# RWKV head products as pairs of 64x64 matmuls on quarters of the array, and both layers written out

## The reference

```python
def step(state, inp):
    r_t, w_t, k_t, v_t, a_t, b_t = inp
    sa = jnp.einsum('bhvk,bhk->bhv', state, a_t)
    state = state * w_t[:, :, None, :] + sa[..., None] * b_t[:, :, None, :] \
            + v_t[..., None] * k_t[:, :, None, :]
    return state, jnp.einsum('bhvk,bhk->bhv', state, r_t)
_, y = lax.scan(step, state0, xs)
```

## Time and profile before

| | us |
|---|---|
| runs: median (lowest to highest of 3) | 1418.83 (1415.55 to 1419.67) |
| profiled execution: span, first to last instruction | 1412.0 |
| PE busy / PEld busy | 1340.1 (95%) / 1273.3 (90%) |
| DVE busy / ACT busy | 885.5 (63%) / 604.4 (43%) |
| mean granted TensorE clock | 0.961 |

### The profile page before, as it was taken

One profiled execution on the slowest core, in us unless ns is written; L12 is line 12 of the kernel. 1 busy time (PEld: TensorE's weight loads), 2 busy tenths in 40 slices (PEclk: granted clock), 3 DMA queues, 4 the chain that ended last, 5 costly groups with the idle time before them and its releaser, 6 DMA issues.

```text
span 1412.0 us, 28243 instructions
## 1 busy us (share of the span) xinstructions
PE 1340.1 (95%) x10414; PEld 1273.3 (90%) x10434; DVE 885.5 (63%) x1518; ACT 604.4 (43%) x904; POOL 47.7 (3%) x31
## 2 busy tenths in 40 slices
PE   7999999979989989999979999999799999999998
PEld 6999998958978879999979999998589788999998
DVE  4666666686653665666656666666866537566665
ACT  3444445545432234444444444455554323344442
POOL 3000000021000000000000000000210000000000
PEclk8999999989999979999989999999899899799999
DMA  5656665510010226665535666655100103366653
GB/s 156 179 179 183 187 184 135 161 57 1 1 45 1 66 86 180 184 185 179 165 109 176 181 185 182 189 130 141 45 2 1 45 1 105 90 182 186 182 179 118
DMA packets 243396, 174.59 MB, mean 124 GB/s; under 512 B 10274, under 2 KB 228540, under 8 KB 243324
## 3 DMA queue, kind: packets, MB, share of 16 engines
q1 hardware_dynamic: 243324, 173.64, 41.6%
HBM read 172.57 MB, written 1.05 MB: 123 GB/s over the span
## 4 chain that ended last, share of the span: by engine, by line
PE 80%; DVE 10%; issue 5%; ACT 2%; DMA 1%; SPq 0%; DVEq 0%; ACTq 0%
PE bank L1294 20%; PE bank L1295 19%; PE bank L1296 19%; PE bank L1565 3%; PE bank L1546 2%; DVE wlo L753 2%; PE bank L1557 2%; PE bank L1311 1%; PE bank L1336 1%; PE bank L1521 1%; PE bank L1301 1%; ACT whi L542 1%; DVE xlo L783 1%; PE bank L1625 1%; DVE root L769 1%
## 5 line engine op out<-in xcount | busy, mean ns | idle before, releaser
L753 DVE TENSOR_TENSOR wlo<-raw,whi 128x1024 fp32r<-128x1024 f32 x324 | 394.7, 1221 | 270.7 <-ACT whi L542 269.4
L1294 PE MATMUL bank<-xhi,whi 128*128 128x256 f32 x1840 | 535.0, 291 | 18.5 <-DVE xlo L783 14.7
L1295 PE MATMUL bank<-xlo,whi 128*128 128x256 f32 x1840 | 527.8, 287 | 0.0
L1296 PE MATMUL bank<-xhi,wlo 128*128 128x256 f32 x1840 | 527.7, 287 | 0.0
L542 ACT ACTIVATE whi<-raw 128x1024 fp32r<-128x1024 f32 x324 | 338.3, 1049 | 299.9 <-PE bank L1296 266.4
L1294 PEld LDWEIGHTS bank<-xhi,whi 128*128 128x128 f32 x1840 | 360.8, 196 | 25.8 <-DVE xlo L783 17.7
L1295 PEld LDWEIGHTS bank<-xlo,whi 128*128 128x128 f32 x1840 | 361.1, 196 | 0.1
L1296 PEld LDWEIGHTS bank<-xhi,wlo 128*128 128x128 f32 x1840 | 360.6, 196 | 0.0
L1294 PE MATMUL bank<-hhi,whi 128*128 128x256 f32 x704 | 202.8, 288 | 0.1
L1295 PE MATMUL bank<-hlo,whi 128*128 128x256 f32 x704 | 201.9, 287 | 0.0
L1296 PE MATMUL bank<-hhi,wlo 128*128 128x256 f32 x704 | 201.7, 287 | 0.0
(11 more groups left out here) (229 smaller groups left out, 1375.1 us busy)
## 6 DMA issues: line engine op xcount, KB each, us to landing
raw<-in_ffn_w_gate_dram SPq DMA_DIRECT2D x88, 512.0 KB, 3.9
raw<-in_ffn_w_up_dram SPq DMA_DIRECT2D x88, 512.0 KB, 3.9
raw<-in_ffn_w_down_dram SPq DMA_DIRECT2D x88, 512.0 KB, 3.3
raw<-in_w_in_dram SPq DMA_DIRECT2D x34, 512.0 KB, 4.0
raw<-in_w_out_dram SPq DMA_DIRECT2D x16, 512.0 KB, 3.4
raw<-in_w_in_dram SPq DMA_DIRECT2D x8, 256.0 KB, 3.2
raw<-in_w_q_up_dram SPq DMA_DIRECT2D x4, 384.0 KB, 3.6
work<-in_x_dram SPq DMA_DIRECT2D x1, 1024.0 KB, 6.6
```

The lines of the kernel that those rows point to most:

```text
L753: V_.tensor_tensor(wlo[:, b.slot, 0:width], raw[:, b.slot, 0:width], whi[:, b.slot, 0:width].bitcast(F32), ALU.subtract).then_inc(lo_ready, 1)
L1294: mm(out, hi, mhi, start=start, stop=False, **kw)
L1295: mm(out, hi, mlo, start=False, stop=False, **kw)
L1296: return mm(out, lo, mhi, start=False, stop=stop, **kw)
```

## The change

In place of one 128x128 matmul with a block-diagonal stationary operand, `both` issues two matmuls of 64x64: partitions 0 to 63 of the operands into partitions 0 to 63 of the PSUM bank, and 64 to 127 into 64 to 127. So the diagonal matrices, their ACT spreads, the pool's compaction of v (vC) and the tensor `pairs` go; the stacks are used as they are. Turning to token-major form becomes a product with a 64x64 identity (`to_tokens`), moved: b stands behind ti1, k inside level 1 and v inside level 2. The copies pc go from DVE to ACT, and the sum of squares `qkss` on DVE goes behind the copies of t0 and b. Layers are a Python loop, so the program holds both bodies; the loops inside the FFNs stay.

```diff
+            def both(out, lhs, rhs, start, stop, **kw):
+                for half in (LO, UP):
+                    ins = mm(out[half], lhs[half], rhs[half], start=start, stop=stop, **kw)
+                return ins
...
-            with pe.Fori(0, DEPTH) as l:
+            for l in range(DEPTH):
...
-            def spread(dst, src, g0=0, n=G):
-                nc.scalar.activation(dst[LO, g0:g0 + n, 0:64], src[LO], ACT.Copy)
-                return nc.scalar.activation(dst[UP, g0:g0 + n, 64:128], src[UP], ACT.Copy)
...
-                            ins = mm(bank[b0 + c][:, P * h:P * (h + 1)], lhs[:, g, :],
-                                     AR[:, g].rearrange("p s i -> p (s i)"), start=True, stop=True)
+                            ins = both(bank[b0 + c][:, P * h:P * (h + 1)], lhs[:, g, :],
+                                       AR[:, g].rearrange("p s i -> p (s i)"), True, True)
...
-                for s, src, b0, wait in (("tb", bP, 0, "g1_"), ("tk", kP, 4, "g2_"), ("tv", vP, 0, "tb")):
-                    for c in range(NC):
-                        pe.wait_ge(mix_dve.sem, mix_dve.at(l, f"{wait}{c}"))
-                        for h in range(HP):
-                            ins = turn(bank[b0 + c][:, P * h:P * (h + 1)], src[:, 4 * c + h, :])
-                        ins.then_inc(mix_pe.sem, mix_pe.step(f"{s}{c}"))
-                pe.wait_ge(mix_act.sem, mix_act.at(l, "tk3"))
-                keep_clock(4, 8)
-                pe.wait_ge(mix_act.sem, mix_act.at(l, "pP"))
-                pe.wait_ge(mix_act.sem, mix_act.at(l, "lP"))
+                def to_tokens(src):
+                    for g in range(G):
+                        ins = both(bank[6 + g // 8][:, 64 * (g % 8):64 * (g % 8 + 1)], src(g), eyes, True, True)
+                    return ins
+                pe.wait_ge(mix_dve.sem, mix_dve.at(l, "p1"))
...
-                            ins = mm(bank[4 + b][:, 64 * j:64 * (j + 1)], lP[:, g, :], tC[:, g, :], start=True,
-                                     stop=True)
+                            ins = both(bank[4 + b][:, 64 * j:64 * (j + 1)], M1[:, g, 0, :], tC[:, g, :], True,
+                                       True)
...
-                                ins = mm(bank[b][:, 64 * j:64 * (j + 1)], pP[:, g, :], uC[:, g, :], start=False,
-                                         stop=k == LEVELS - 1, skip_group_check=True)
+                                ins = both(bank[b][:, 64 * j:64 * (j + 1)], pC[:, g, :], uC[:, g, :], False,
+                                           k == LEVELS - 1, skip_group_check=True)
...
-                    pe.wait_ge(mix_act.sem, mix_act.at(l, f"ub{c}"))
-                    if c:
-                        pe.wait_ge(mix_act.sem, mix_act.at(l, f"sb{c - 1}"))
...
-                        mm(o, vP[:, g, :], M2[:, g, 1, :], start=True, stop=False)
-                        ins = mm(o, uP[:, 4 * (c % 2) + h, :], M1[:, g, 1, :], start=False, stop=c == 0)
+                        both(o, v_tok[:, g, :], M2[:, g, 1, :], True, False)
+                        ins = both(o, rec[:, 1, h, :], M1[:, g, 1, :], False, c == 0)
```

More of the change, by code:

```diff
@@ L293, in build @@
         work = sb("work", [P, 16, 1024])
-        pairs = sb("pairs", [P, 7, G, P])
+        gram = sb("gram", [P, 2, 2, G, C])
+        tokens = sb("tokens", [P, 3, G, C])
+        solved = sb("solved", [P, G, C])
+        qk_sq = sb("qk_sq", [P, 3072])
         def unit(i, n=1):
@@ L311, in build @@
         bC, kC = stacks(14), stacks(15)
[L313 to L318, removed]
+        M1, M2 = (gram[:, i].rearrange("p s g i -> p g s i") for i in range(2))
+        b_tok, k_tok, v_tok = (tokens[:, i] for i in range(3))
+        tC, pC, uC = stacks(0), stacks(7), stacks(1)
         rec = unit(3).rearrange("p (s h i) -> p s h i", s=4, h=HP)
-        yT, yN, ysc, scrap = unit(4), unit(5), unit(8), unit(7)
+        yT, yN, ysc, scrap = unit(4), unit(5), unit(8), unit(8)
         parts = unit(7, 2)
-        aP, bP, kP, vP, lP, pP, uP = (pairs[:, i] for i in range(7))
         lat = unit(3)[:, 0:768].rearrange("p (t n) -> p t n", t=3)
@@ L485, in flat @@
                 return v.rearrange("a p n -> p (a n)")
-            with sp.Fori(0, DEPTH) as l:
+            for l in range(DEPTH):
                 sp.dma_start(rows1[:],
@@ L670, in mixing @@
                 act.wait_ge(mix_dve.sem, mix_dve.at(l, "qe3"))
[L671 to L683 removed]
+                nc.scalar.activation(qk_sq[:], unit(3, 3), ACT.Square).then_inc(mix_act.sem, mix_act.step("qksq"))
                 ahead(len(RW_TILES) + 7), ahead(len(RW_TILES) + 8), ahead(len(RW_TILES) + 9)
@@ L736, in mixing @@
                     ahead(i)
-            with act.Fori(0, DEPTH) as l:
+            for l in range(DEPTH):
                 ffn(l, 0)
@@ L1067, in mixing @@
                     V_.tensor_copy(eight(tC, b), bank8(b)).then_inc(mix_dve.sem, mix_dve.step(f"t0_{b}"))
+                dve.wait_ge(mix_pe.sem, mix_pe.at(l, "tb"))
+                for b in range(2):
+                    ins = V_.tensor_copy(eight(b_tok, b), bank8(6 + b))
+                ins.then_inc(mix_dve.sem, mix_dve.step("tb"))
+                dve.wait_ge(mix_act.sem, mix_act.at(l, "qksq"))
+                V_.tensor_reduce(stat[:, 0:32], qk_sq[:].rearrange("p (g d) -> p g d", d=QK), AX_X,
+                                 ALU.add).then_inc(mix_dve.sem, mix_dve.step("qkss"))
+                dve.wait_ge(mix_dve.sem, mix_dve.at(l, "qkss"))
                 q3 = unit(3, 3).rearrange("p (g d) -> p g d", d=QK)
@@ L1274, in _ @@
                                bank[i][:]).then_inc(x_ready, 1)
-            with dve.Fori(0, DEPTH) as l:
+            for l in range(DEPTH):
                 dve.wait_ge(mix_pe.sem, mix_pe.at(l, "prm1"))
```

144 lines of the change are left out of this document (50 added, 94 removed).

## The result

The changed kernel takes 1329.11 us (median; 1327.90 to 1343.68 in 4 runs), the kernel before on the same chip 1417.19 (1414.64 to 1419.67 in 4 runs). The ratio, estimated from all the runs, is 0.9418, 95% interval 0.9375 to 0.9461 (the two medians alone give 0.938). The profiled execution of the changed kernel took 1329.74 us, its span is 1328.0 at a mean granted clock of 0.976; before it was 1412.0 at 0.961. So 84.0 us of span are to be found, where the sum had 53.7. A single execution lies 1.7 to 1.8 us above its span, as here; the rest of the 6.8 us that the forecast put between the two was the distance of one profiled execution from the median.

What follows compares the result with a forecast made beforehand. PE, almost without a gap, was taken to bound the mixing stages, so only cheaper matmuls help. Levels 18.4, recurrence 9.2, less 2 for clock, twice, plus 2.5 gave 53.7 off 1412.0; plus 6.8, 1365 us, range 1343 to 1440 (forecast's own 1343 to 1390).

Steps and rivals of the forecast that it cites:

- the sum: Whole kernel: 2 x (18.4 + 9.2 - 2) + 2.5 = 53.7 us off the span of 1412.0, giving 1358.3.
- the 6.8 us: Median of the runs above the span of the profiled execution; added to the span of 1358.3 to give 1365.
- A pair of quarter matmuls: Two overlapping 64x64 matmuls cost 0.134 us against 0.224 for one block-diagonal matmul; bounds 0.112 and 0.448.
- The fixed 0.014 a pass slot: Overhead of each pass, from fp32r matmuls, added to 0.053 for a pass slot of 0.067 us.
- the rivals at 0.18, 0.212, 0.224 and 0.448: Pair costs in us: partial overlap, chance 0.18; load and matmul in turn, 0.03; quarters in turn, 0.14; size without effect, 0.05.
- Before the levels: g1 to b's turn: Gram passes take 7.7 us, then PE idles 3.4 us ahead of ti0, waiting for p1 on DVE.
- The clock after the pause: From ti0 on: a clock fall after the idle 3.4 us costs 2 us a layer, bounds 0 and 6.
- The levels: Stretch to qkT: cheaper pairs put qkT at 376.0 against 394.42, 18.4 us gained a layer, with DVE waits in levels 1 and 3.
- The recurrence: x, u, s and y of four chunks: 112 matmuls at 0.09 us less, 10.1 us a layer, net 9.2 after corrections.
- The two corrections of the sum: Recurrence: 1.6 us lost to DVE's late copy of x in chunk 1; 0.82 gained as chunk 3's y skips ACT.
- Layers written out: Layer boundary: without PE's backward branch, DVE's parameter copy comes earlier, 2.5 us gained once, bounds 0 and 5.
- The low end of the range: 1343 us, with 0.05 left below it; a pair at 0.112 gives 1347.

Runs made afterwards that it cites:

- the run with the clock kept: Changed kernel with 13 matmuls of zeros in PE's pause ahead of ti0: 1332.93 us, ratio 0.9421.
- the changed kernel with both edits: Changed kernel with zeros in the pause ahead of ti0 and the sum of qk_sq moved ahead of the copies of t0: 1334.01 us, ratio 0.9414.
- The kernel before with its pauses filled: Kernel before, layers written out, zeros in attention's second pause and between the waits of each FFN's first down block: 1396.52 us, ratio 0.9885.

## Why the prediction came out too high

**A pair of quarter matmuls.** Taken at 0.134 us, measured at 0.120 (13.45 us for 448 passes) and 0.117 in the recurrence, near the lower end of 0.112. The fixed 0.014 a pass slot, carried over from fp32r matmuls, is 0.005 to 0.007 here: two passes, one on each quarter, every 0.058 to 0.060. That the quarters overlap was the choice on which everything hung, and it holds; the rivals at 0.18, 0.212, 0.224 and 0.448 fall. "TensorEngine Tiling (Array Packing)" of the Trainium skill, Gotcha 1, would have the two quarters exclude each other, since both write one bank. The traces disagree: their passes start 0.01 us apart, and a pair takes 0.120 of 0.224. The quarters here lie on the diagonal, and write different partitions of the bank.

**Before the levels.** g1 and g2: forecast 7.7, measured 7.22. The 64 pairs of 128 moving columns gain nothing over 7.41, as forecast. Pause ahead of ti0: 3.4, measured 3.17. ti0 and ti1: 3.96, measured 4.34 at whole clock. The clock after the pause: 2 taken, between 0 and 6; 2.7 in layer 0, none in layer 1.

**The levels.** t of level 1 started 24.8 us behind g1 in layer 0 and 22.1 in the run with the clock kept, forecast 22.9; PE waits there for the mask behind the 3.35 us sum, as it said, and moving the sum shows that wait to be real. The next 14 groups of eight pairs: 15.0 forecast, 13.45 measured. In level 3 PE waits for tc0 behind the gains (3.47 us), as forecast; 4.8 us from the end of the chain's PE part to the next u, forecast 5.3. Level 4 and u of level 5: 8.6, measured 7.78. Together, at whole clock, 22.2 us a layer (72.1 to 49.95) where 18.4 was forecast. Most of the 3.8 is the pair (1.55 us of it in the 14 groups and 0.8 in level 4 and u of level 5).

**The recurrence.** 9.2 a layer forecast, 9.2 measured at whole clock in both. The two corrections of the sum are there: PE idles 1.40 us ahead of u of chunk 1 because DVE's copy of x stands behind the normalization of y, and chunk 3 has no wait for ScalarE. The forecast period of 6.9 is between the 7.69 of chunks 1 to 2 and the 6.26 of chunks 2 to 3. The agreement is in part luck: with the pair as measured, 112 x (0.224 - 0.117) = 12.0 in place of 10.1, the same sum would give 11.2, so 2 us a layer are lost somewhere that it doesn't have, and no run says where.

**Layers written out.** 2.5 forecast, 3.5 measured in the profile (3.4 in the kernel before with this edit alone). Both boundaries also have 3 us less at half clock, so up to 1.7 of it can be clock, which the part's upper bound had allowed for.

**The step that failed** is the sum's: "2 x (18.4 + 9.2 - 2) + 2.5". It holds the clock only as a cost of one new pause, and puts at nothing the time that the old kernel spent at half clock elsewhere. That kernel had 109.2 us of its span at half clock, being one such stretch, and the changed kernel 64.9. With the terms as measured at whole clock the sum is 2 x (22.2 + 9.2) + 3.5 - 2.7 = 63.6 of the 84.0. The remaining 20.4 lie in stretches that the change doesn't touch, or beyond its work there: from qkT to the means 23.8 - 18.4 = 5.4, the way into FFN 2 9.7, the FFN loops 5.2, the start 0.8, less 0.7 before the mask. The first three are clock: they have 13.6, 24.0 and 13.5 us less at half clock. The 0.8 of the start are not, since both profiles have 10.2 to 10.3 us at half clock there. Work at half clock takes up to twice its time (1.98 us for 0.961), so 44.3 us less of it in all can give up to 22.2.

The 20.4 belong to this pair of profiles. Against the second profile of the changed kernel (92.2 us at half clock, span 1334.9) the same stretches give 16.4. How much of this the change brings every time and how much is the moment's is not shown; both profiles of before (109.2 and 105.8) lie above both of after, but the changed kernel with both edits, whose matmuls are the same, has 101.4.

The other misses are smaller. The levels were put at 18.4 for 22.2, the new pause at 4 for 2.7 and the boundary at 2.5 for 3.5: 9.9 us together, which alone would have left the time at 1355, inside the range. And the 6.8 us from the span to the median was the chance distance of one execution; in the changed kernel it is 1.1, which makes 5.7 of the 35.9 us between 1365 and 1329.

Two checks from the other side. The kernel before with its pauses filled and as little half clock as the changed one needs 58.3 us more in the stretches that the change touches, where the sum has 2 x (22.2 + 9.2) = 62.8 at whole clock and the changed kernel's profile loses 5.1 of them to half clock. And the earlier trace rows was in the prediction, read as a warning for a new pause and not as time that the old kernel could lose. The low end of the range came from the pair alone (0.112 gives 1347), so nothing in it covered this term.

**What stays open** is why the changed kernel is granted more clock at its FFN entries. It is not the written-out loop (the kernel before with it has 110.2 us at half clock). It can be had by filling pauses, so it is the clock and not the work. In profiles with small edits upstream, copies that nobody reads or zeros in another place, 3 to 4 us of it are gone again in one layer or both, but each is one profile, and no run here isolates what brings the clock down there.

## What to carry to other kernels

Two 64x64 products on diagonal quarters, issued in turn, took 0.120 us where the block-diagonal f32 one took 0.224, where the load of the stationary operand set the pace, and gained nothing at 128 moving columns. They must alternate: one quarter after the other cost 0.335 us a pair for 0.25 at half clock, and held the stretch at half clock, so that the kernel became slower than with the whole array. Before summing the terms of a change, add up the kernel's time at half clock: it is a term of its own, which fell by some 16 to 20 us here in stretches that nobody had edited, and came back in part with edits elsewhere. A saving of 2 to 5 us found in one stretch is not a saving until the total shows it.

## What the runs showed of the hardware that was not expected

- PE busy without a gap on mostly one quarter at a time was granted 0.50 over 47 us, and the clock stayed there for 105.8 us in a layer; with matmuls on both diagonal quarters and 30.30 of 33 us busy it was granted 1.00.
- Two quarters of f32 passes write different partitions of one PSUM bank at once: 0.120 us a pair of 64x64 with 64 columns at full clock, 0.25 at half, where one quarter alone makes a pass every 0.107 us and would need 0.43.
- With 128 moving columns a pair takes 7.22 / 32 = 0.226 us, and the block-diagonal matmul took 7.41 / 32 = 0.232.
- The same program spends 64.9 or 92.2 us of its span at half clock in two profiles, and their spans are 1328.0 and 1334.9 us.
